# The norm of k in a hybrid encoder block: a power of -1/2 on GpSimd in place of a root on ScalarE and a reciprocal on VectorE

## The reference, cut to what matters

```python
kk = (k * k_k).reshape(B, T, H, N).astype(f32)
kk = kk / jnp.maximum(jnp.sqrt(jnp.sum(kk * kk, axis=-1, keepdims=True)), L2_EPS)   # L2_EPS = 1e-12
k = k * (1.0 + (a - 1.0) * k_a)
...
xs = (both_dirs(rh), dec, both_dirs(kh), both_dirs(vh),
      both_dirs(-kk), both_dirs(kk * ah.astype(f32)))      # inputs of the scan, one per direction
```

## Time and profile before

| | |
|---|---|
| median of 3 runs | 1827.09 us (1822.47 to 1831.57) |
| the profiled execution's own time | 1828.29 us |
| its span | 1826.2 us |
| busy: PE, DVE, ACT, POOL | 85%, 44%, 26%, 3% of the span |

### The profile page before, as it was taken

How to read it: one execution, slowest core, us unless ns; L and a number is a source line. 1 busy time by engine, 2 the same in 40 slices (tenths; PEclk the granted TensorE clock), 3 DMA queues, 4 the chain that set the end, 5 groups by cost and what they waited for, 6 DMA issues and landing times.

```text
span 1826.2 us, 27591 instructions
## 1 busy us (share of the span) xinstructions
PE 1552.1 (85%) x11156; PEld 1143.8 (63%) x11156; DVE 798.3 (44%) x975; ACT 479.6 (26%) x694; POOL 46.0 (3%) x45
## 2 busy tenths in 40 slices
PE   0897898989388988778639969999999999999994
PEld 0345445454166766556518748888878888878883
DVE  4254736679045454455571363332223332223335
ACT  2132341310033333344421233221012221022221
POOL 0000000011000000000020000000000000000000
PEclk9998998989667787778769979999999999999997
DMA  4007255273744443453211101111111111111112
GB/s 158 26 32 179 75 135 152 62 188 81 180 136 117 118 119 101 120 144 97 53 56 57 46 23 46 51 53 46 46 47 46 46 46 58 46 46 46 38 43 92
DMA packets 186992, 148.31 MB, mean 81 GB/s; under 512 B 100464, under 2 KB 166128, under 8 KB 184784
## 3 DMA queue, kind: packets, MB, share of 16 engines
q1 hardware_dynamic: 182672, 136.48, 26.6%
q0 software_dynamic: 1728, 5.64, 1.1%
q10 hardware_dynamic: 2560, 5.77, 1.0%
HBM read 106.04 MB, written 41.81 MB: 81 GB/s over the span
## 4 chain that ended last, share of the span: by engine, by line
PE 74%; DVE 11%; SPq 6%; issue 4%; ACT 3%; DMA 3%; DVEq 0%; ACTq 0%
PE banks L474 44%; PE banks L462 13%; PE banks L606 3%; PE banks L595 2%; PE banks L651 2%; PE banks L541 2%; ACT work L871 2%; DVE work L1167 2%; PE banks L481 1%; PE banks L586 1%; SPq L324 1%; DVE work L1149 1%; PE banks L666 1%; DVE hT L1013 1%; PE banks L673 1%
## 5 line engine op out<-in xcount | busy, mean ns | idle before, releaser
L462 PE MATMUL banks<-hT,work 128*128 128x512 f32 x640 | 281.8, 600 | 28.4 <-issue 17.5
L474 PE MATMUL banks<-h_hi,w_hi 128*128 128x512 f32 x832 | 259.7, 394 | 29.1 <-DVE h_lo L994 14.1
L474 PE MATMUL banks<-h_lo,w_hi 128*128 128x512 f32 x832 | 258.2, 392 | 0.0
L474 PE MATMUL banks<-h_hi,w_lo 128*128 128x512 f32 x832 | 258.0, 391 | 0.0
L462 PEld LDWEIGHTS banks<-hT,work 128*128 128x128 f32 x640 | 122.2, 192 | 185.8 <-issue 177.4
L474 PEld LDWEIGHTS banks<-h_hi,w_hi 128*128 128x128 f32 x832 | 157.1, 190 | 66.3 <-issue 29.6
L885 ACT ACTIVATE w_hi<-work 128x1024 fp32r<-128x1024 f32 x76 | 80.2, 1057 | 384.5 <-PE banks L474 384.5
L474 PEld LDWEIGHTS banks<-h_lo,w_hi 128*128 128x128 f32 x832 | 157.7, 190 | 33.1
L474 PEld LDWEIGHTS banks<-h_hi,w_lo 128*128 128x128 f32 x832 | 157.4, 189 | 33.0
L1258 DVE TENSOR_TENSOR xT<-xT,banks 128x1024 f32<-128x1024 f32 (+1 forms) x32 | 39.1, 1221 | 240.7 <-PE banks L474 240.7
L474 PE MATMUL banks<-g_hi,w_hi 128*128 128x512 f32 x352 | 108.4, 389 | 0.0
(11 more groups left out here) (156 smaller groups left out, 1764.0 us busy)
## 6 DMA issues: line engine op xcount, KB each, us to landing
work<-in_w_gu SPq DMA_DIRECT2D x44, 512.0 KB, 3.5
work<-in_w_in SPq DMA_DIRECT2D x20, 512.0 KB, 3.3
AR_d<-work SPq DMA_DIRECT2D x8, 1024.0 KB, 5.4
G_d<-work SPq DMA_DIRECT2D x8, 1024.0 KB, 5.1
BK_d<-work SPq DMA_DIRECT2D x32, 256.0 KB, 5.7
work<-AR_d SPq DMA_DIRECT2D x32, 256.0 KB, 3.4
work<-G_d SPq DMA_DIRECT2D x32, 256.0 KB, 3.8
work<-BK_d SPq DMA_DIRECT2D x32, 256.0 KB, 3.9
```

What stands on the lines that cost most here:

```text
L462: mm = pe.matmul(out[:, h * HALF:(h + 1) * HALF], wt[:, k, :], src[:, k, h * HALF:(h + 1) * HALF], start=(k == 0), stop=(k == kn - 1))
L474: mm = pe.matmul(out[:, h * HALF:(h + 1) * HALF], wp[slot][:, k, :], xp[:, k, h * HALF:(h + 1) * HALF], start=(k == 0 and p_ == 0), stop=( ...
```

## The change

The root leaves ScalarE. VectorE takes the maximum straight from `ps[1]`, on the squared sum and with the squared bound, and does so ahead of the shift of r. GpSimd raises the result to -0.5, elementwise and in place, with a constant column broadcast over 1024 elements as its second input; in its queue this stands ahead of the two products for `BK`. VectorE waits for the power where it had the maximum and the reciprocal.

```diff
+        neg_half = w(1)
@@ ScalarE
                 own_share(1, rT, 3)
-                act.wait_ge(s["ss_mm"], j + 1)
-                act.activation(sqT, ps[1], ACT.Sqrt).then_inc(s["nrm_ready"], 1)
                 own_share(2, vT, 0)
@@ GpSimd
+            pool.memset(neg_half, -0.5).then_inc(s["half_made"], 1)
+            pool.wait_ge(s["half_made"], 1)
             with pool.Fori(0, NPAIR) as j:
+                pool.wait_ge(s["nrm_ready"], j + 1)
+                pool.tensor_tensor(sqT, sqT, neg_half.broadcast_to([P, T]), ALU.pow).then_inc(s["kk_rsq"], 1)
                 for z in range(2):
                     pool.wait_ge(s["kp_ready"], j + 1)
@@ VectorE
                 tt(kT, kT, tpT, ALU.mult).then_inc(s["kp_ready"], 1)
 
+                dve.wait_ge(s["ss_mm"], j + 1)
+                ts(sqT, ps[1], L2_EPS * L2_EPS, None, ALU.max).then_inc(s["nrm_ready"], 1)
                 shift(1, rT, 3)
...
                 stt(tpT, rT, col("r_k", j), kT, ALU.mult, ALU.mult).then_inc(s["bon_in"], 1)
 
-                dve.wait_ge(s["nrm_ready"], j + 1)
-                ts(sqT, sqT, L2_EPS, None, ALU.max).then_inc(s["nrm_max"], 1)
-                dve.wait_ge(s["nrm_max"], j + 1)
-                dve.reciprocal(sqT, sqT).then_inc(s["nrm_rec"], 1)
-                dve.wait_ge(s["nrm_rec"], j + 1)
+                dve.wait_ge(s["kk_rsq"], j + 1)
                 stt(kkT, kkT, -1.0, sqT, ALU.mult, ALU.mult).then_inc(s["nk_ready"], 1)
```

More of the change, by code:

```diff
@@ L217, in hymba_block @@
             p_mm p_scaled p_shift1 p_shifted lora_tanh gate_sig lw_full
-            dz0_mm dz1_mm ic_mm sig0 sig1 a_ready kk_ready kk_sq ss_mm nrm_ready nrm_max nrm_rec nk_ready b_ready
+            dz0_mm dz1_mm ic_mm sig0 sig1 a_ready kk_ready kk_sq ss_mm nrm_ready kk_rsq nk_ready half_made b_ready
             ka_fac kp_ready bon_in bon_mm bon_out vt_mm vts_ready v_stored
```

## The result

The changed kernel takes 2452.31 us (median of 4 runs, 2448.44 to 2452.94) against 1829.33 us (1822.47 to 1831.79, 4 runs) of the kernel before: 1.341 times the time, 95% interval 1.337 to 1.345. The forecast was 1899 us with a range up to 2010. The direction was right and the size was far off: 623 us slower, where 71 were forecast.

A forecast was written before the change was run, and what follows sets the result against it. VectorE, late by 2.3 to 2.65 us per pair with PE right behind, was taken as the bound. Delay 17.0 plus 0.7 us cold PE, 17.7 per pair, 71 for four, on 1828.3 gave 1899 us; range 1822 to 2010.

The forecast's parts named there:

- What bounds the stretch: Pair loop before the Gram products: VectorE is late by 2.3 to 2.65 us per pair, with PE right behind.
- ScalarE's part at nothing: Removing ACT's root (1.02 us) and table load (1.28 us) gains nothing, covered by its 12.01 us wait for v.
- The duration of the power: GpSimd's power per pair: T = 23.2 us, as two hard functions at 5.35 plain passes of 2.17 us; ends 2.17 and 46.4.
- The contention: Shared SBUF access holds L1072 1.28 us past the power; the BK product adds 2.17: 3.45 us before L1079.
- T - 6.2: Forecast delay D of a pair's Gram products in us, T being the power's duration; 17.0 us with T = 23.2.
- PE standing cold: Gram products run slower after PE's idleness: 0.7 us more per pair.
- Nothing absorbs the delay: Behind the Gram products, what direction 0 gains or loses the pair gains or loses; 71 us for four pairs.
- The rival of the other side: Rival 1: power nearly as cheap as a product, VectorE's relief counts; 9.7 us gained, 1819 us; chance 0.06.
- a slower way: Rival 3, much slower power: T = 46.4, 1992 us, slower still if worked lane by lane; chance 0.27.
- the prediction's form: Loss per pair: delay T - 6.2 us plus 0.7 us for cold PE, taken over four pairs.
- the point of change: Power duration T below which the change would gain: forecast at 6.2 us.

## Why the prediction was wrong, step by step

- **What bounds the stretch: right.** VectorE was late by 2.3 to 2.65 us with PE right behind. The experiments that free VectorE gain about 4 us per pair, which is the gap and 1.55 us of clock, and not their full 6.55 or 7.23 us.
- **ScalarE's part at nothing: right.** Root and table load are gone from each pass, which has three table loads in place of four, and ScalarE's wait for the projection of v grew from 12.01 to 14.34 us.
- **The duration of the power: this step failed.** It was put at 2 x 5.35 x 2.17 = 23.2 us, with 46.4 us as the upper end. It is 163.2 us, 75 plain passes and 7.0 times the estimate. The ratio 5.35 was that of VectorE's reciprocal to its plain pass, carried over to another engine. Nothing in the trace tied the two, and the upper end was a multiple of the same guess and no bound. The text said of a slower way that no row bounds it, and yet gave everything above 2010 us only a third of 0.27.
- **The contention: half right.** The forecast held L1072 to the end of the power and put 3.45 us between the power and the norm's product. In fact L1077, the same instruction, is let in with 512 elements left, long before the end, so only the 2.15 us product for `BK` stays: L1080 took 3.19 us in place of 1.22, 2.0 us more. That makes the delay T - 7.7 and not T - 6.2.
- **PE standing cold: right on average, with luck.** 0.7 us was put in, from a gap of 5.07 us. The first Gram products of the four pairs take 6.66, 6.13, 5.27 and 6.49 us, against 5.50, 5.43, 5.50 and 5.50 before: 0.65 us more on average, but 0.2 less to 1.2 more in single pairs.
- **Nothing absorbs the delay: right.** With the measured T the prediction's form gives (163.2 - 6.2 + 0.7) x 4 = 631 us, against a span longer by 624.3. With the contention as it is, (155.5 + 0.65) x 4 = 625.
- **The rival of the other side: right in mechanism, too small.** The gain was put at 9.7 us and the point of change at T = 6.2 us. The runs show 15.6 to 18.8 us and 7.7 us. What the gain lacked is the clock: Gram products that follow at once take 3.95 us and not 5.50. The point of change was put too low by the contention, 3.45 us in place of 2.0.

By the floor for two-input arithmetic in the GPSIMD Engine Reference of the Trainium skill (section 3.1), cited in the prediction, 1024 elements would take 2.2 us, which is an estimate. The product for `BK`, with 2.17 us, agrees; the product with a broadcast column took 1.89 us, somewhat under it, and the power's 163.2 us are far off: that floor said nothing about its price. By the lock rule of the Trainium skill's page SBUF — State Buffer (section Who interferes with whom) L1077 would have ended after the power, at 286 us or later; the trace has 205.65. The rule held for the product with a scalar beside a power and for L1080 beside the product for `BK`, and not for an instruction with two inputs beside a power.

## What to carry to other kernels

An operation that no row of the profile shows has no upper bound from the rows of other operations: measure it alone before it goes on a path, or let the range say that its price is open by a factor of ten. An operation of GpSimd is not cheap because the engine is idle: the power costs 0.159 us per element of a row, however many partitions it covers, so on the whole tile it is dear; only under some 48 elements per row would it have gained in this kernel. An idle stretch of an engine that can do the step cheaply is worth a look: ScalarE made the whole norm in its wait for the projection of v. Where an engine waits just short of its neighbour, closing the gap can give more than the gap, since TensorE then keeps its clock.

## What the runs showed of the hardware that was not expected

- A power on GpSimd takes 0.4 us and 0.159 us per element of the row: 163.22, 81.92, 20.72 and 0.55 us for widths of 1024, 512, 128 and 1. One partition costs as much as 128 (20.7 us at width 128), and exponent, base and operand form change that by at most 0.1 us.
- VectorE instructions with two SBUF inputs were kept out of a running power until 512 elements were left (83.4 us into 163.2, 164.7 into 244.5, not at all beside 512 and 256). A product with a scalar was kept out to the end of the power, and L1080, with two SBUF inputs, to the end of GpSimd's product for `BK`.
- The 128 Gram matmuls of the first direction take 3.95 us at a granted clock of 1.00 when PE comes from work or from 0.35 us of idleness, 5.50 us after 2.65 us of it, and 5.27 to 6.66 us after some 85 us.
- Logarithm and exponential in a row on ScalarE made two table loads, 1.28 us each.
